# A gated delta recurrence on four quarters of the matmul array, with half columns, moved vector work, and row products for the first norm

## The reference, cut to what matters

```
sk = einsum('bhij,bhj->bhi', S, kkt)
S = S * wt[:, :, None, :] - sk[..., None] * bt[:, :, None, :] + vt[..., None] * kt[:, :, None, :]
y = einsum('bhij,bhj->bhi', S, rt)
```

## Time and profile before

| | |
|---|---|
| median of three runs | 3206.38 us |
| profiled execution | 3205.18 us, of which the span is 3203.4 us |
| PE, DVE, ACT, POOL busy | 3109.8, 2230.5, 572.8, 225.5 us |
| recurrence, first level of pass 0 to first chunk step of pass 12 | 608.62 to 1054.72 us |
| two passes (odd and even) in its steady part | 77.44 us |
| first FFN product starts | 47.02 us |

### The profile page before, as it was taken

The page is one execution under the profiler, slowest core; times in us unless marked ns, Lnnn a source line. Parts: engine busy times, 40 slices in busy tenths (PEclk is TensorE's granted clock), DMA queues, the critical chain, the costliest instruction groups (busy, mean ns, idle before and its releaser), DMA issues.

```text
span 3203.4 us, 64602 instructions
## 1 busy us (share of the span) xinstructions
PE 3109.8 (97%) x27984; PEld 2866.3 (89%) x27984; DVE 2230.5 (70%) x4724; ACT 572.8 (18%) x1157; POOL 225.5 (7%) x240
## 2 busy tenths in 40 slices
PE   7999999899999999999999999999999999999999
PEld 3888875588888899999899999999899999999998
DVE  6887967666676477675757666786677676786675
ACT  2000010234333211111121011141110102230111
POOL 1000010122222010000000000010000000000000
PEclk9999999999999999999999999999999999999999
DMA  7456665100000255455345564334345442344353
GB/s 296 159 222 245 248 235 215 45 7 7 7 6 7 80 171 173 170 172 186 107 150 172 201 230 141 124 136 156 123 169 177 173 158 106 135 143 165 132 171 119
DMA packets 68653, 467.50 MB, mean 146 GB/s; under 512 B 7232, under 2 KB 9920, under 8 KB 14105
## 3 DMA queue, kind: packets, MB, share of 16 engines
q1 hardware_dynamic: 51120, 369.12, 32.8%
q0 software_dynamic: 12192, 87.04, 7.4%
q10 hardware_dynamic: 5065, 7.27, 0.8%
HBM read 457.64 MB, written 5.77 MB: 145 GB/s over the span
## 4 chain that ended last, share of the span: by engine, by line
PE 91%; DVE 6%; ACT 1%; issue 1%; DMA 0%; POOL 0%; ACTq 0%; DVEq 0%; POOLq 0%
PE ps L918 32%; PE ps L1445 18%; PE ps L973 8%; PE ps L1590 4%; PE ps L1000 4%; PE ps L1032 4%; PE ps L774 2%; PE ps L1070 1%; PE ps L1083 1%; PE ps L1089 1%; PE ps L852 1%; PE ps L1464 1%; PE ps L1520 1%; PE ps L1389 1%; PE ps L1494 1%; PE ps L1344 1%
## 5 line engine op out<-in xcount | busy, mean ns | idle before, releaser
L918 PE MATMUL ps<-arena 128*128 128x128 f32 x4328 | 510.6, 275 | 0.0
L918 PEld LDWEIGHTS ps<-arena 128*128 128x128 f32 x4328 | 496.7, 192 | 0.0
L918 PE MATMUL ps<-arena,ring 128*128 128x128 f32 x2176 | 270.3, 275 | 0.0
L2108 DVE TENSOR_TENSOR arena<-arena,ps 128x256 f32<-128x256 f32 x143 | 60.2, 421 | 282.6 <-ACT arena L1658 258.3
L918 PEld LDWEIGHTS ps<-arena,ring 128*128 128x128 f32 x2176 | 256.4, 192 | 0.0
L2253 DVE CUSTOM_DVE_ANT_0 arena<-arena,vec 128x1024 f32<-128x1024 f32 x168 | 206.6, 1280 | 1.6 <-DMA arena<-in_ada_t 1.6
L1445 PE MATMUL ps<-y,arena 128*128 128x128 f32 x1560 | 191.1, 278 | 5.0 <-DVE arena L2060 5.0
L1445 PEld LDWEIGHTS ps<-y,arena 128*128 128x128 f32 x1560 | 182.5, 194 | 8.8 <-DVE arena L2060 5.2
L2073 DVE TENSOR_TENSOR arena<-ring 128x512 f32<-128x512 f32 (+1 forms) x167 | 112.3, 672 | 53.7 <-DMA ring<-in_w_f_down 26.2
L1445 PE MATMUL ps<-h,ring 128*128 128x128 f32 x1040 | 128.4, 276 | 0.8 <-ACT h L1994 0.8
L1445 PEld LDWEIGHTS ps<-h,ring 128*128 128x128 f32 x1040 | 124.0, 192 | 3.2 <-issue 1.0
(11 more groups left out here) (451 smaller groups left out, 6057.8 us busy)
## 6 DMA issues: line engine op xcount, KB each, us to landing
ring<-in_w_f_gu SPq DMA_DIRECT2D x88, 1024.0 KB, 4.8
arena<-in_ada_t POOLq DMA_DIRECT2D x72, 1024.0 KB, 6.2
ring<-in_w_f_down SPq DMA_DIRECT2D x48, 1024.0 KB, 4.9
ring<-in_w_fx_gu SPq DMA_DIRECT2D x44, 1024.0 KB, 4.8
ring<-in_w_fx_down SPq DMA_DIRECT2D x24, 1024.0 KB, 4.8
ring<-in_w_qk_a SPq DMA_DIRECT2D x18, 1024.0 KB, 4.9
ring<-in_w_qk_r SPq DMA_DIRECT2D x16, 1024.0 KB, 4.8
ring<-in_w_v_r SPq DMA_DIRECT2D x16, 1024.0 KB, 4.7
```

Of the source, the lines that this page charges most:

```text
L918: last = mm(out, weights[number][:, j * P:(j + 1) * P], inputs[number](base + j), start=(s.opens and j == 0 and number in (1, 5)), stop=(s ...
```

## The change

- **Four quarters.** In the X products the second head of a pair writes to the other half of the partitions (`facing`), and to a PSUM bank of its own; `x_sb` and `tri_t` hold that head crosswise. So `level_x`, the first half of `level_t`, `halves_x` and `halves_t` address four quarters (`halves` and the last level two instead of one).
- **Half columns.** `level_t` makes only the 32 columns of 64 that change (`moved`, `blocks`), and `level_done` subtracts only these: 128 x 256 in place of 128 x 512. The X products and their copy keep their size.
- **Features.** Two decay products use rows 0-63 and two use rows 64-127, not 128 rows with zeros; the product with `blk` becomes two of 64 x 64; the gate's product moves to slot 3.
- **Moved.** `key_rate` and `scaled_key` go from DVE to ACT. The scan, its subtractions and the rest of the preparation go to other slots; `exponents` stays in slot 2 of even passes, ahead of `x_copy` of level 2, and `key_rate` comes behind it. DVE does `minus_u(1)` ahead of slot 4. `first_blocks`, `masked_lat` and `masked_mix` of the next unit come behind `joined`, with `chunk_out(3)` between the masks. For odd units `first_level` goes from slot 11 to 12. `strict` comes ahead of `keys_tok` for even units. `own_blocks` goes to the end of ACT's pass, as four copies, not two.
- **First norm.** Scales and shifts are both products on PE, with a stationary operand of 32 columns (2 in use) and results in four strips of 32 partitions (`row_products`), one copy of 128 x 512, and 8 products that add the strips and turn them (`row_columns`). DVE's 16 sums go, and the broadcast of the conditioning vector is loaded after the shift rows.

```diff
+        cond_k = take(KD, 32)
+        pick = take(2, 2)
...
+        LAT_BANK, MIX_BANK = (7, 3), (4, 6)
+        UP_BANK = (3, 4, 7, 6)
...
+        def facing(hd, rows):
+            return rows if hd == 0 else (SECOND if rows == FIRST else FIRST)
...
-            pool.dma_start(cond.rearrange("p a b -> p (a b)"), A["cond"].to_broadcast([P, 2 * D])).then_inc(cond_in, 16)
...
+            pool.wait_ge(shift_landed[ADA_SHIFT - 1], 16)
+            pool.dma_start(cond.rearrange("p a b -> p (a b)"), A["cond"].to_broadcast([P, 2 * D])).then_inc(cond_in, 16)
...
+            def row_products(name, landing, rows, bank):
+                for j in range(KD):
+                    if j % 2 == 0:
+                        pe.wait_ge(landing[j // 2], 16)
+                    for half in range(2):
+                        at = 32 * (2 * (j % 2) + half)
+                        last = mm(ps[at:at + 32, bank, :], cond_k[:, j], rows[:, j // 2, j % 2, 512 * half:512 * half + 512],
+                                  start=(j < 2), stop=(j >= KD - 2))
+                last.then_inc(*step(f"pe.{name}"))
...
+                    if c == 0:
+                        pe.wait_ge(*past(f"act.{name}"))
+                    for half in range(2):
+                        k = 4 * half + c
+                        last = mm(ps[:, bank, 2 * k:2 * k + 2], shift_rows[:, c * P:(c + 1) * P], pick[:, half], start=True, stop=True)
...
+            row_products("scales", ada_landed, ada_ring, 0)
+            pe.wait_ge(*past("dve.pick"))
+            row_columns("scales", 2)
+            row_products("shifts", shift_landed, ada_shifts, 6)
+            row_columns("shifts", 5)
...
+            def head_sums(out, x):
+                for rows in (FIRST, SECOND):
+                    last = mm(out[rows], ones[rows, 0:64], x[rows], start=True, stop=True)
+                return last
...
-                for hd in range(2):
-                    for c in range(4):
+                for c in range(4):
+                    for hd in range(2):
                         for rows in (FIRST, SECOND):
-                            last = mm(ps[rows, 0, at(hd, c)], am[rows, lev % 2, hd, c], tri[rows, q, hd, c],
+                            last = mm(ps[facing(hd, rows), hd, cols(c)], am[rows, lev % 2, hd, c], tri[rows, q, hd, c],
                                       start=True, stop=True)
...
-                for hd in range(2):
-                    for c in range(4):
+                for c in range(4):
+                    for hd in range(2):
                         for rows in (sides(u)[:1] if lev == LEVELS - 1 else (FIRST, SECOND)):
-                            last = mm(ps[rows, 0, at(hd, c)], tri_t[rows, q, hd, c], x_sb[rows, hd, c],
-                                      start=True, stop=True)
+                            held = facing(hd, rows)
+                            last = mm(blocks(ps[rows, hd, c * 32:c * 32 + 32], lev), tri_t[held, q, hd, c],
+                                      moved(x_sb[held, hd, c], u, lev, 0), start=True, stop=True)
                 last.then_inc(*step(f"pe.t{u}_{lev}"))
...
-                            last = mm(ps[rows, 1, at(hd, c)], x_sb[rows, hd, c], tri_t[rows, q, hd, c],
-                                      start=True, stop=True)
+                            out = (4 * hd + c) * 32
+                            last = mm(blocks(ps[rows, TWIN, out:out + 32], lev), x_sb[rows, hd, c],
+                                      moved(tri_t[rows, q, hd, c], u, lev, 1), start=True, stop=True)
...
-                for hd in range(2):
-                    for c in range(4):
-                        last = mm(ps[hi, 0, at(hd, c)], n_off[lo, q, hd, c], tri[lo, q, hd, c], start=True, stop=True)
+                for c in range(4):
+                    for hd in range(2):
+                        last = mm(ps[facing(hd, hi), hd, cols(c)], n_off[lo, q, hd, c], tri[lo, q, hd, c], start=True, stop=True)
...
-                for hd in range(2):
-                    for c in range(4):
-                        last = mm(ps[lo, 1, at(hd, c)], x_sb[hi, hd, c], tri_t[hi, q, hd, c], start=True, stop=True)
+                for c in range(4):
+                    for hd in range(2):
+                        held = facing(hd, hi)
+                        last = mm(ps[lo, (TWIN, 0)[hd], cols(c)], x_sb[held, hd, c], tri_t[held, q, hd, c],
+                                  start=True, stop=True)
...
-                    pe.wait_ge(*past(f"dve.k_mix{2 * t - 1}"))
-                for n in range(4):
-                    mm(ps[:, 3 + n, :], ups[:, n, :], z_a[:, 18, :], start=True, stop=True) \
+                    pe.wait_ge(*past(f"dve.k_lat{2 * t - 1}"))
+                for n in (0, 2, 1, 3):
+                    if n == 1 and t:
+                        pe.wait_ge(*past(f"dve.k_mix{2 * t - 1}"))
+                    rows = (FIRST, SECOND)[n // 2]
+                    mm(ps[:, UP_BANK[n], :], ups[rows, n, :], z_a[rows, 18, :], start=True, stop=True) \
                         .then_inc(*step(f"pe.up{t}_{n}"))
-                mm(ps[:, 7, 0:SEQ], ups[:, 4, :], z_a[:, 19, 0:SEQ], start=True, stop=True).then_inc(*step(f"pe.up{t}"))
...
+                mm(ps[:, 6, 0:SEQ], ups[:, 4, :], z_a[:, 19, 0:SEQ], start=True, stop=True).then_inc(*step(f"pe.up{t}"))
...
-                            last = mm(ps[rows, 7, at(hd, c)], am[rows, 0, hd, c], eye64[rows], start=True, stop=True)
+                            last = mm(ps[rows, 1, at(hd, c)], am[rows, 0, hd, c], eye64[rows], start=True, stop=True)
...
                     elif n == 9:
+                        strict(u)
+                    elif n == 10:
                         keys_tok(u)
-                    elif n == 10:
-                        strict(u)
...
-                    elif n == 11:
+                    elif n == 12:
                         first_level(u)
...
+            act.wait_ge(cond_in, 16)
+            f(cond, cond, ACT.Silu).then_inc(*step("act.cond"))
...
-                rows = slice(0, P) if lev < LEVELS else sides(u)[1]
-                f(flat(x_sb)[rows], ps[rows, 0, :], ACT.Copy).then_inc(*step(f"act.x{u}_{lev}"))
+                if lev < LEVELS:
+                    last = f(by_chunk(x_sb), by_head(), ACT.Copy)
+                else:
+                    for hd in range(2):
+                        rows = facing(hd, sides(u)[1])
+                        last = f(by_chunk(x_sb)[rows, hd], ps[rows, hd, 0:256], ACT.Copy)
+                last.then_inc(*step(f"act.x{u}_{lev}"))
...
+            def key_rate(u):
+                d, t = u % 2, u // 2
+                act.wait_ge(*past(f"act.sig{t}"))
+                act.wait_ge(*past("dve.mus"))
+                if unit(u - 1):
+                    act.wait_ge(*past(f"dve.kt{u - 1}"))
+                    act.wait_ge(*past(f"dve.kdsum{u - 1}"))
+                f(kd, rate[:, d], ACT.Identity, scale=V("k_a", t), bias=omka[:, t:t + 1]).then_inc(*step(f"act.kd_a{u}"))
+            def scaled_key(t):
+                act.wait_ge(*past(f"dve.kk{t - 1}_6"))
+                act.wait_ge(*past(f"dve.kr{2 * t - 1}"))
+                f(kkr, z_a[:, 6 + t, :], ACT.Copy, scale=V("k_k", t)).then_inc(*step(f"act.kkr{t}"))
...
+                    elif n == 4:
+                        key_rate(u)
                     elif n == 6:
                         exponents(u)
                         if u == 0:
                             fourier_out()
                     elif n == 9:
+                        strict_copies(u)
+                    elif n == 10:
                         tok_copies(u)
...
                 elif unit(u):
                     if n == 2:
                         exponents(u)
+                        key_rate(u)
...
-                        if unit(p):
-                            own_blocks(p)
                     fill(p, 2 * lev)
+                    if lev == LEVELS and unit(p):
+                        own_blocks(p)
...
-            adaln(ADA_FIRST)
-            gain_of(0, 0)
...
+            v.wait_ge(*past("act.n0_std"))
+            nc.vector.reciprocal(rs[:], rs[:]).then_inc(*step("dve.n0_rstd"))
...
+                if k == 1:
+                    rows_to_columns("shifts", 5, 0).then_inc(*step("dve.n0_shift"))
+            v.wait_ge(*past("act.cond"))
...
-                tt(eight(tri[rows, q]), eight(tri[rows, q]), four_eight(0)[rows], ALU.subtract) \
+                own = tri[rows, q].rearrange("p h c (b two s) -> p h (c b) two s", two=2, s=2 ** lev)[:, :, :, u % 2]
+                tt(own, own, by_head(P)[rows].rearrange("p h (b s) -> p h b s", s=2 ** lev), ALU.subtract) \
                     .then_inc(*step(f"dve.t{u}_{lev}"))
                 v.wait_ge(*past(f"pe.tt{u}_{lev}"))
-                tt(eight(tri_t[:, q]), eight(tri_t[:, q]), four_eight(1), ALU.subtract).then_inc(*step(f"dve.tt{u}_{lev}"))
+                own = moved(tri_t[:, q].rearrange("p h c t -> p (h c t)"), u, lev, 1)
```

(64 more changed lines are left out.)

158 lines of the change are left out of this document (90 added, 68 removed).

## The result

The changed kernel takes 3308.51 us (median of 4, 3308.41 to 3320.71), the kernel before 3206.31: a ratio of 1.033, 95% interval [1.031, 1.035]. The forecast of 3181 was wrong in sign. The profiled execution took 3308.41 us with a span of 3306.5.

A forecast was written before the change was run, and what follows sets the result against it. PE, busy 97% of the span, was taken as the bound. Odd passes -18.5, even +6.5, pass 0 -3.0, pass 11 -5.8 and first norm -4.2 gave -25 from 3205.2, a median of 3181 us; range 3152 to 3195.

The forecast's parts named there:

- First norm: Start of the kernel: row products in four strips take 3.5 us, first FFN product starts at 42.8, 4.2 us earlier.
- Four quarters and features: Recurrence on PE: 12 products a pass shorten to 0.69 or 0.63 us, 5.5 less; features 1.8 less in odd passes.
- Rival 3: `level_x`, `level_t`, `halves`: crosswise second head doesn't run beside the first, products keep 1.15 us; +44, 3225; chance 0.09.
- the new waits: Recurrence: PE waits from the new order, priced from 0.3 to 3.7 us each and added to each pass.
- half columns: Second half of `level_t`: no PE time saved, 1.1 us a product kept; DVE's subtractions 2.6 us less a pass.
- a wait of 3.7 us: Even pass: PE idles 3.7 us before t of level 2, behind ACT's exponents, `key_rate` and `x_copy`.
- The bounds given: Half-column products in `level_t`: 1.1 us each or half of it, 0.5 less each; the upper bound was taken.
- The odd pass: Steady odd pass of the recurrence: 37.4 us against 41.08, 3.7 shorter, new waits included.
- the even one: Steady even pass of the recurrence: 37.7 us against 36.36, 1.3 longer, because of the new waits.
- Pass 0: First pass of the recurrence: 3.0 us shorter, DVE's chain losing 2.6 and gaining a wait before `chunk_rhs(0)`.
- rival 5: Recurrence: nothing comes of the change there, further waits of 2 us a pass eat the gain; 3201; chance 0.08.
- Rival 1: Even passes: clock falls to 1.2 GHz after 3.7 us idle, 1.8 lost in each of five; +9, 3190; chance 0.16.

The follow-up runs named there:

- e2: Changed kernel with idle PE products put into its new waits, nothing else changed: 3211.5 us, ratio 1.0027.
- e13: Changed kernel with the half columns undone (full columns in a level's products and DVE's subtractions), timed in rounds: 3245.7 us, ratio 1.013.
- e14: Kernel before with the half columns alone, its two quarters and order kept: 3216.3 us, ratio 1.0035.
- e5: Kernel before, with ACT copying X of level 2 seven times in even passes, so PE waits some 3.6 us before level 2's products: 3234.6 us.
- e12: The short-waits kernel e7 with idle PE products in the waits behind which its clock still fell: 3131.6 us, ratio 0.976.
- e7: Changed kernel with four placements put back and its last long waits removed by reordering, four quarters and half columns kept: 3146.9 us, ratio 0.981.
- e16: e12 with full columns in a level's products and in DVE's subtractions: 3138.8 us.
- e15: Kernel before with half columns and the added wait of e5 before level 2's products in even passes: 3242.0 us.
- e8: e7 with the second head of a pair not crosswise, so a level's products use two quarters: 3186.1 us.

## Why the prediction was wrong

**Where the 102 us are.** By spans: changed 3306.5, e2 3200.2, before 3203.4. The first norm gives 5.4, the recurrence in e2 loses 2.2 (3200.2 - 3203.4 + 5.4), and covering the waits gives 106.3 (97 by the medians: the profiled execution of e2 was the fastest of ten). The 106 need both the waits and the half columns. With the waits covered and the half columns kept, all of it comes back (e2); with full columns and the waits kept, 63 comes back (e13, span 3243.3). The two can't be added up.

**First norm: right**, 5.4 for 4.2. The strips took 3.64 where 3.5 was forecast; the rest is that they started at 27.2, not at the 28.3 from which the sum counted.

**Four quarters and features: right.** 0.69 and 0.67 us a product, features 1.99 (1.9). Rival 3 fell by these rows: crosswise halves run side by side.

**The steps that failed: the new waits were priced at their own length, at full clock, and the half columns "on PE" at nothing.** In the forecast's sum a wait of 3.7 us costs 3.7 us; the clock behind it is in no term. The runs show some 106 us there (e2). The half columns are the second step. A product's duration is as forecast, 1.10 us. But its price on PE is not only its duration: at half the columns the clock stays down once it has fallen (63 us come back with full columns, e13), and in the kernel before it even falls without a long wait (e14: 11 us slower than the kernel before). No row of the kernel before could show it, since all its columns were full. The bounds given, half or nothing, had no end above nothing, and nothing in the profile excluded one.

**The sizes of the new waits: right one by one, short in the sum for the even pass.** 0.70 (0.8), 0.88 (0.8), 4.36 (3.7), 2.0 to 2.4 (2.1), 2.53 (2.1), `strict` 2.0 in e13 (2.1). The odd pass was forecast at 37.4 and is 37.30 in e2; the even one at 37.7 and is 40.63. Missing is the wait of 1.53 before the last `chunk_rhs`: DVE's y copy of slot 9 now stands behind the reciprocal and four more operations of the readout, since slot 7's work moved behind `minus_u(2)`. The rest is the 0.7 of t of level 2 and smaller ones. Pass 0 was forecast 3.0 shorter and is 1.0 longer (29.79 for 28.80 in e2). So even without the clock the gain would have been small: less some 6 us for its three falls in steady passes, e2 stands at 3196, as an estimate from its passes. Of the 25 us of the forecast some 9 are left; 13 went in the even passes and 4 in pass 0. That is most of the way to rival 5's 3201, by its mechanism, though in the even passes only.

**Rival 1: right in kind, a tenth of the size.** Its step was "If each of five even passes runs as long at 1.2 GHz as those four products did". Three things in it were wrong. It counted five falls; there were 22, in odd passes too, though two waits of 2.1 were forecast there by the same text. It took 3.68 us for the length, from a place with wide, dense products behind it; here stretches last 4 to 22 us in the steady passes and 45 at the end, through pass 11 and into pass 12. And it laid its loss of 9 us over a gain of which the waits had already eaten two thirds. The Trainium skill (TensorE: Matmul & The Clock Gate, Part 1) says that the clock is set by how busy the engine has lately been. The trace agrees for the starts (e2, e5), but what the profile calls busy is not what counts: PE was busy 6.00 of 6.00 us at 1.2 GHz in the changed kernel, and e14's clock fell without a long wait.

**The range** (3152 to 3195) took in this rival at its price of 9 us only, and no case in it had the clock low for more than a few us a pass.

## What to carry to other kernels

When a change makes products on PE shorter or narrower, look at what stands between them: the same shorter products came with +102 us in one order and with -74 in another (e12, with idle products in its waits; -59 without them, e7). Price each new wait with the clock behind it, in every pass, and test it by putting idle products into the wait: if the kernel gets faster, it is the clock. Before halving the columns of products whose duration does not fall, ask what that buys on the other engines, since here it bought 7 us with the clock up (e12, e16) and cost 63 where waits brought it down (changed, e13).

## What was not expected of the hardware

- The same wait before the products of the same level was followed in the steady passes by 4 us at 1.2 GHz when they moved 64 columns and by 8 to 11 when they moved 32, with PE busy in both (e5, e15, passes 4 to 10); and after a wait of 2.5 us in the changed kernel by 21.
- Idle products of 0.12 us an instruction, which wrote 128 columns each with a 128-column stationary operand, kept the clock up in most waits of 1.5 to 4.4 us (e2: 24 us at 1.2 GHz in place of 299).
- Left open: why e14, whose steady passes have no wait over 0.9 us, falls in four of ten of them and for 35 us in pass 0. Half columns alone don't do it: e8, with half columns, two quarters and no idle products, stays at 1.00 in all ten (39 us at 1.2 GHz in all, 35 of them in pass 0 again), and e7, with four quarters, in the odd ones from pass 3 on. PE waits less in e8's steady passes, 0.4 at the longest and 0.5 to 0.9 in sum from pass 3 on, where e14 has 1.2 to 1.7. But e7's odd passes have 1.95 in sum, with a wait of 0.80 that no idle product covers. No run separates the order, the waits and the quarters here.
